# The retention layer's gate projection as seven half-size products per weight block, laid between the heads' products

## The reference, cut to what matters

```python
z = hn @ od_w_in[j]
q, k, v, g = _split(z, OD_SPLIT)          # widths 1024, 1024, 2048, 2048
...
    inner = jnp.einsum("bihd,bjhd->bhij", qc, kc) * decay_intra[None]
    o_inner = jnp.einsum("bhij,bjhe->bihe", inner, vc)
...
o = ((o - mu) * lax.rsqrt(var + GN_EPS)).reshape(b_, s_, h_ * dv) * gn_g.astype(jnp.float32)
y = jax.nn.silu(g.astype(jnp.float32)) * o
...
mix = yc @ od_w_out[j]
h = h + mix
h = h + hier_moe(rms_norm(h, ffn_norm_g[i]), ...)
```

## Time and profile before

| | |
|---|---|
| time, median of 3 runs | 1332.78 us (1332.29 to 1334.24) |
| the profiled execution: time, span of its instructions | 1333.76 us, 1332.0 us |
| PE busy | 1051.0 us (79%) |
| DVE busy | 439.2 us (33%) |
| ACT, POOL busy | 177.8 us (13%), 91.9 us (7%) |
| chain that ended last | DMA 49%, PE 45%, DVE 2% |
| all DMA | 474.88 MB, mean 357 GB/s |

### The profile page before, as it was taken

One profiled execution on the slowest core, in us unless ns is written; L12 is line 12 of the kernel. 1 busy time (PEld: TensorE's weight loads), 2 busy tenths in 40 slices (PEclk: granted clock), 3 DMA queues, 4 the chain that ended last, 5 costly groups with the idle time before them and its releaser, 6 DMA issues.

```text
span 1332.0 us, 26354 instructions
## 1 busy us (share of the span) xinstructions
PE 1051.0 (79%) x10946; PEld 625.6 (47%) x10946; DVE 439.2 (33%) x914; ACT 177.8 (13%) x418; POOL 91.9 (7%) x228
## 2 busy tenths in 40 slices
PE   6999987666676667769999999988666766766678
PEld 5885444333343334434688554544333333333343
DVE  1698522112111111226674547423111211111117
ACT  2334311001000000012121000221000000000011
POOL 0110011000000000000110000011000000000000
PEclk9999999888888888899999999999888888888899
DMA  9945899999999999999454336799999999999992
GB/s 357 322 172 222 336 412 425 429 429 427 430 427 431 428 430 429 427 418 380 167 188 142 113 126 241 300 419 426 430 427 428 429 428 430 427 430 428 427 423 105
DMA packets 57840, 474.88 MB, mean 357 GB/s; under 512 B 4056, under 2 KB 6104, under 8 KB 32192
## 3 DMA queue, kind: packets, MB, share of 16 engines
q1 hardware_dynamic: 56800, 470.32, 85.6%
q10 hardware_dynamic: 768, 2.57, 0.5%
q0 software_dynamic: 224, 1.31, 0.3%
HBM read 473.12 MB, written 3.16 MB: 358 GB/s over the span
## 4 chain that ended last, share of the span: by engine, by line
DMA 49%; PE 45%; DVE 2%; issue 1%; ACT 1%; SPq 1%; POOL 0%; DVEq 0%; ACTq 0%; POOLq 0%
DMA big<-in_moe_w_up_dram 49%; PE ps L935 10%; PE ps L675 7%; PE ps L1121 5%; PE ps L700 5%; PE ps L666 3%; PE ps L1034 3%; PE ps L745 2%; PE ps L656 2%; PE ps L957 1%; PE ps L965 1%; PE ps L846 1%; SPq L540 1%; PE ps L863 1%; DVE big L1797 0%
## 5 line engine op out<-in xcount | busy, mean ns | idle before, releaser
L935 PE MATMUL ps<-big 128*32 128x256 f32 x4064 | 321.7, 484 | 160.1 <-DMA big<-in_moe_w_up_dram 159.9
L935 PEld LDWEIGHTS ps<-big 128*32 128x32 f32 x4064 | 165.9, 138 | 310.6 <-issue 182.4
L1793 DVE SCALAR_TENSOR_TENSOR big<-big,ps 64x256 f32<-64x256 f32 x64 | 26.4, 413 | 682.1 <-ACT big L1356 682.1
L957 PE MATMUL ps<-big 128*32 128x256 f32 x2048 | 123.8, 382 | 57.7 <-DVE big L1802 57.7
L957 PEld LDWEIGHTS ps<-big 128*32 128x32 f32 x2048 | 59.9, 109 | 107.9 <-DVE big L1802 74.8
L965 PE MATMUL ps<-big 32*128 32x256 f32 x1024 | 73.3, 398 | 41.8 <-ACT big L1367 40.6
L1356 ACT ACTIVATE big<-ps 64x256 f32<-64x256 f32 x64 | 24.1, 377 | 566.6 <-PE ps L935 566.6
L675 PE MATMUL ps<-big,xT 128*128 128x512 f32 x224 | 98.1, 592 | 0.0
L965 PEld LDWEIGHTS ps<-big 32*128 32x128 f32 x1024 | 49.5, 184 | 70.8 <-issue 70.8
L2228 POOL TENSOR_TENSOR big<-big,rk 128x64 f32<-128x64 f32 x64 | 18.8, 294 | 769.1 <-PE ps L944 741.9
L905 PE MATMUL ps<-xn,big 128*32 128x256 f32 x1056 | 69.3, 379 | 0.0
(11 more groups left out here) (253 smaller groups left out, 1031.5 us busy)
## 6 DMA issues: line engine op xcount, KB each, us to landing
big<-in_moe_w_gate_dram SPq DMA_DIRECT2D x64, 2048.0 KB, 33.1
big<-in_moe_w_down_dram SPq DMA_DIRECT2D x62, 2048.0 KB, 38.6
big<-in_moe_w_up_dram SPq DMA_DIRECT2D x60, 2048.0 KB, 37.3
big<-in_od_w_in_dram SPq DMA_DIRECT2D x12, 2048.0 KB, 13.4
big<-in_ev_w_in_dram SPq DMA_DIRECT2D x6, 2048.0 KB, 20.7
big<-in_ple_w_gate_dram SPq DMA_DIRECT2D x8, 1024.0 KB, 22.2
big<-in_od_w_out_dram SPq DMA_DIRECT2D x4, 2048.0 KB, 7.9
big<-in_moe_w_up_dram SPq DMA_DIRECT2D x6, 1024.0 KB, 35.5
```

Source lines behind the costliest of these rows:

```text
L935: ins = nc.tensor.matmul(ps[TOK * i:TOK * i + TOK, 5, 0:2 * P].rearrange("p (b n) -> p b n", b=2), xe[:, k, :], (low if k < KD // 2 else w ...
L957: ins = nc.tensor.matmul(ps[TOK * q:TOK * q + TOK, 7, 0:QD], hidT[:, k, :], wd[:, k, q * QD:(q + 1) * QD], start=k == 0, stop=k == KF - 1)
```

## The change

1. Each gate block is computed by the same seven products as the blocks of `SEVEN`: `rg{c}_a` and so on, each four matmuls of 256 columns. In the first of a block's two head steps stand `a, b, d`, in the second `c, a2, b2, c2`. `rg0_a` and `rg0_b` stand ahead of the loop.
2. `GATE_LAG` and `BACK_LAG` become 1 and 3, so the loop has 11 steps, not 12.
3. Banks are fixed in the loop: 4 to 7 for the gate products, 0 for every `ret`, 1 and 2 for `ro`, 3 (and once 0) for `yT`.
4. VectorE gets four weight differences per block. `rg_first` stands behind the value products, `rg_second` between a head's statistics and its scaling, the other two at the end of the block's first step. `rg_part` and `rg_sums` add the products. The gated rows of a block move to the first step of the next block, one half ahead of the head's scaling and one behind it, and now read both operands from SBUF.
5. ScalarE copies four products per block out of PSUM and makes tanh from SBUF.
6. `S4` moves to another place, since it must live through the loop. `S1` to `S3` stay.
7. The first tile and sums of the output projection are made in the loop's step 9, behind the last gated rows.

```diff
+RG_STEPS = ("a", "b", "d"), ("c", "a2", "b2", "c2")
...
-GATE_LAG, BACK_LAG = 2, 4
+GATE_LAG, BACK_LAG = 1, 3
...
+    jobs += ["rg0_a", "rg0_b"]
...
-        jobs += [f"rg{n // 2}_{n % 2}"] if 0 <= n < NH else []
+        jobs += [f"rg{n // 2}_{i}" for i in RG_STEPS[n % 2] if n or i == "d"] if 0 <= n < NH else []
...
+        fixed |= {f"rg{c}_{i}": 4 + "abdc".index(i[0]) for c in range(4) for i in PRODUCTS}
+        fixed |= {f"ret{i}": 0 for i in range(NH)} | {f"ro{i}": 1 + i % 2 for i in range(NH)}
+        fixed |= {f"yT{c}_{t}": 0 if (c, t) == (3, 1) else 3 for c in range(4) for t in range(NT)}
+        fixed |= {f"last_{i}": b for i, b in zip("abdc", (4, 6, 7, 1))} | {"rout_00": 5, "gain1": 2}
...
-            following = 4 if name == "ret0" else following
...
-        S4 = view(15872, HALF, P)
+        S4 = pT[:, 0, :, :].rearrange("p k s -> p (k s)").rearrange("p (k s) -> p k s", k=HALF)
+        RT2 = view(4096, HALF, VD)
+        rg_kept = [[view(12288 + VD * i, VD) for i in range(4)]] + [[view(o1, VD) for o1 in (5120, 5376, 7168, 7424)]] * 3
...
+            RELEASE[f"rv{c}"], RELEASE[f"rg{c}"] = f"rv{c}_c2", f"rg{c}_c2"
...
+            def rg_product(c, i):
+                B11, T1, B21, B22 = rg_quarters(c)
+                lhs, rhs = {"a": (A11, B11), "b": (S1, T1), "d": (S2, RT2), "c": (S3, B11), "a2": (A12, B21), "b2": (S4, B22),
+                            "c2": (A22, T1)}[i]
+                tiles = {"b": c + 1, "d": 5 + 3 * c, "c": 6 + 3 * c, "c2": 7 + 3 * c}
+                b = begin(f"rg{c}_{i}")[:, 0:VD]
+                if i in tiles:
+                    pe.wait_ge(rg_tiles, tiles[i])
+                for k in range(HALF):
+                    ins = nc.tensor.matmul(b, lhs[:, k, :], rhs[:, k, :], start=k == 0 and len(i) == 1, stop=k == HALF - 1,
+                                           skip_group_check=True)
+                end(f"rg{c}_{i}", ins)
+            arrived("rg0")
+            rg_product(0, "a")
+            rg_product(0, "b")
             for w in ROTATED:
                 for t in range(NT):
                     taken(pe, f"{w}T_{t}")
...
-                    c, t = divmod(hd - GATE_LAG, 2)
-                    tokens([f"rg{c}_{t}"], slot(arrived(f"rg{c}"), KD, BLK), t)
+                    c, part = divmod(hd - GATE_LAG, 2)
+                    arrived(f"rg{c}")
+                    for i in RG_STEPS[part]:
+                        if (c, i) not in ((0, "a"), (0, "b")):
+                            rg_product(c, i)
...
-            for n in range(8):
-                if n >= 2:
-                    act.wait_ge(gtanh_used, n - 1)
-                name = f"rg{n // 2}_{n % 2}"
-                full(act, name)
-                sc.activation(rota[:, n % 2, 0, :], bank(name), ACT.Tanh, scale=0.5).then_inc(gtanh_ready, 1)
+            act.wait_ge(values_ready, 5)
+            for c in range(4):
+                P1c, P5c, P7c, _ = rg_kept[c]
+                for i, dst in (("a", P1c), ("b", P5c), ("c", P7c)):
+                    copy_out(f"rg{c}_{i}", dst, bank(f"rg{c}_{i}")[:, 0:VD])
+                if c:
+                    act.wait_ge(ret_y_ready, 2 * c - 1)
+                copy_out(f"rg{c}_a2", rota[:, 0, 1, 0:VD], bank(f"rg{c}_a2")[:, 0:VD])
+                taken(act, f"rg{c}_a2")
+                taken(act, f"rg{c}_b2")
+                sc.activation(rota[:, 0, 0, :], rota[:, 0, 1, :], ACT.Tanh, scale=0.5).then_inc(gtanh_ready, 1)
+                taken(act, f"rg{c}_c2")
+                act.wait_ge(rg_corner, c + 1)
+                sc.activation(rota[:, 1, 0, :], rota[:, 1, 1, :], ACT.Tanh, scale=0.5).then_inc(gtanh_ready, 1)
...
+            def rg_first(c):
+                dve.wait_ge(landed[loads.at[f"rg{c}"]], 16 * loads.turn[f"rg{c}"])
+                B11, B12, B21, B22 = rg_quarters(c)
+                ve.tensor_tensor(B12, B12, B11, ALU.subtract).then_inc(rg_tiles, 1)
+            def rg_second(c):
+                B11, T1, B21, B22 = rg_quarters(c)
+                dve.wait_ge(rg_tiles, 4 + 3 * c)
+                ve.tensor_tensor(RT2, B22, T1, ALU.subtract).then_inc(rg_tiles, 1)
+            def rg_third_and_fourth(c):
+                B11, T1, B21, B22 = rg_quarters(c)
+                dve.wait_ge(rg_tiles, 5 + 3 * c)
+                full(dve, f"rg{c}_a")
+                ve.tensor_tensor(B11, RT2, B11, ALU.subtract).then_inc(rg_tiles, 1)
+                full(dve, f"rg{c}_b")
+                ve.tensor_tensor(T1, B21, RT2, ALU.subtract).then_inc(rg_tiles, 1)
+            def rg_part(c):
+                P1c, _, _, U2 = rg_kept[c]
+                taken(dve, f"rg{c}_a")
+                full(dve, f"rg{c}_d")
+                emptied(f"rg{c}_d", ve.tensor_tensor(U2, P1c, bank(f"rg{c}_d")[:, 0:VD], ALU.add))
+            def rg_sums(c):
+                _, P5c, P7c, U2 = rg_kept[c]
+                taken(dve, f"rg{c}_b")
+                taken(dve, f"rg{c}_c")
+                v(ve.tensor_tensor(P5c, P5c, P7c, ALU.add))
+                taken(dve, f"rg{c}_d")
+                v.sync()
+                ve.tensor_tensor(rota[:, 1, 1, VD:2 * VD], U2, P5c, ALU.add).then_inc(rg_corner, 1)
+                for i, dst in (("b2", rota[:, 0, 1, VD:2 * VD]), ("c2", rota[:, 1, 1, 0:VD])):
+                    full(dve, f"rg{c}_{i}")
+                    emptied(f"rg{c}_{i}", ve.tensor_tensor(dst, U2, bank(f"rg{c}_{i}")[:, 0:VD], ALU.add))
+            def gated_rows(c, t):
+                dve.wait_ge(gtanh_ready, 2 * c + t + 1)
+                v(ve.scalar_tensor_tensor(out=rota[:, t, 1, :], in0=rota[:, t, 0, :], scalar=1.0, in1=rota[:, t, 1, :],
+                                          op0=ALU.add, op1=ALU.mult))
+                for g in (2 * c, 2 * c + 1):
+                    taken(dve, f"ro{g}")
+                cols = ro[:, t, c * 512:(c + 1) * 512]
+                v.sync()
+                ve.tensor_tensor(cols, cols, rota[:, t, 1, :], ALU.mult).then_inc(ret_y_ready, 1)
...
+                else:
+                    rg_first(m - 2)
...
+            rg_second(0)
             for hd in range(HEAD_STEPS):
+                block_n, part = divmod(hd - GATE_LAG, 2)
...
+                if part == 0 and block_n > 0:
+                    gated_rows(block_n - 1, 0)
+                if part == 1 and 0 <= block_n < 3:
+                    rg_second(block_n + 1)
+                if 0 < hd <= NH:
                     dve.wait_ge(gn_root, g + 1)
...
-                n = hd - GATE_LAG
-                if 0 <= n < NH:
-                    c, t = divmod(n, 2)
-                    name = f"rg{c}_{t}"
-                    dve.wait_ge(gtanh_ready, n + 1)
-                    emptied(name, ve.scalar_tensor_tensor(out=rota[:, n % 2, 1, :], in0=rota[:, n % 2, 0, :],
-                                                          scalar=1.0, in1=bank(name), op0=ALU.add, op1=ALU.mult))
-                    taken(dve, name)
-                    dve.sem_inc(gtanh_used, 1)
-                    for g in (2 * c, 2 * c + 1):
-                        taken(dve, f"ro{g}")
-                    cols = ro[:, t, c * 512:(c + 1) * 512]
-                    ve.tensor_tensor(cols, cols, rota[:, n % 2, 1, :], ALU.mult).then_inc(ret_y_ready, 1)
-                if hd == NH:
+                if part == 0 and block_n > 0:
+                    gated_rows(block_n - 1, 1)
+                if part == 0 and block_n < 4:
+                    rg_third_and_fourth(block_n)
+                    rg_part(block_n)
+                if part == 1 and 0 <= block_n < 4:
+                    rg_sums(block_n)
+                if hd == NH + GATE_LAG:
                     out_arrived("rout0", "rout1")
                     out_tile(1, 0, 0)
-                if hd == NH + GATE_LAG:
                     out_parts(0)
                 n = hd - BACK_LAG
                 if 0 <= n < NH:
```

More of the change, by code:

```diff
@@ L362, in trunk @@
         out_read = sem("out_read")
+        rg_tiles, rg_corner = sem("rg_tiles"), sem("rg_corner")
         bank_full = [sem(f"bank_full{i}") for i in range(BANKS)]
@@ L413, in trunk @@
         gn_ready, gn_root = sem("gn_ready"), sem("gn_root")
-        gtanh_ready, gtanh_used, ret_y_ready = sem("gtanh_ready"), sem("gtanh_used"), sem("ret_y_ready")
+        gtanh_ready, ret_y_ready = sem("gtanh_ready"), sem("ret_y_ready")
         ro_ready = sem("ro_ready")
@@ L469, in trunk @@
         for c in range(4):
-            RELEASE[f"rv{c}"], RELEASE[f"rg{c}"] = f"rv{c}_c2", f"rg{c}_1"
+            RELEASE[f"rv{c}"], RELEASE[f"rg{c}"] = f"rv{c}_c2", f"rg{c}_c2"
         for c in range(2):
@@ L479, in quarters, with rg_quarters @@
             w = held(loads.at[SEVEN[m]], KD, BLK)
+            return [w[:, HALF * i:HALF * i + HALF, VD * j:VD * j + VD] for i in range(2) for j in range(2)]
+        def rg_quarters(c):
+            w = slot(f"rg{c}", KD, BLK)
             return [w[:, HALF * i:HALF * i + HALF, VD * j:VD * j + VD] for i in range(2) for j in range(2)]
```

## The result

The changed kernel takes 1326.24 us, median of four runs (1324.2 to 1326.81), against 1332.8 for four runs of the kernel before (1332.29 to 1334.24): a ratio of 0.9946, 95% interval 0.9929 to 0.9964. It is faster, as forecast, by more than the 5.3 us forecast: 6.6 by the medians, 7.2 by the ratio (4.8 to 9.5). Taken together with the rounds of e1 and e2, 13 timings of the kernel before and 9 of the change have means of 1332.5 and 1326.4: 6.1 us apart, give or take 1.

What follows compares the result with a forecast made beforehand. TensorE's queue was taken to bound 729.4 to 853.7, full DMA engines the second mixture. TensorE's 6.6 less 1.0 lost in block 0 and 0.3 later gave 5.3: 1332.78 to 1327.5 us, range 1325.9 to 1330.0.

Steps and rivals of the forecast that it cites:

- That TensorE's time passes to the end: Whatever TensorE saves between 729.4 and 853.7 moves SyncE's last loads, the full DMA stretch and the end equally.
- the rival in which the saving is absorbed: Loads, not TensorE, decide when the DMA engines are full, so nothing moves: 1332.8; absorbed or nearly, chance 0.09.
- TensorE's work, 6.6: Gate blocks in the head steps: seven half-size products cost 12.09 instead of 13.74 us, 6.6 less over four blocks.
- The queue of bank waits, 0.3: Ahead of `ret0`: some twenty semaphores to wait on, costing TensorE 0.3 us, bounds 0 and 0.4.
- `ret1`, 1.0: Block 0: `ret1` waits 1.0 us for bank 0, until VectorE's inner of `ret0` is done.
- `rg0_c`, 0.8 to 1.0: Block 0: `rg0_c` waits 0.8 to 1.0 us for the third weight difference, made only after `ro0`'s scaling.
- The waits in blocks 1 to 3, 0.3: TensorE's waits for VectorE's third difference in the later blocks, 0.3 us in all, with GpSimd's root not hidden.
- Nothing added, VectorE ahead throughout: Rival: no waits in blocks 1 to 3, saving 5.6 to 6.0, time 1327.0; within the forecast's range, no separate chance.
- the rule that the prediction took from the Trainium skill: VectorE and GpSimd share a port pair, locked for a whole instruction when the VectorE one has two SBUF inputs.
- The lead: VectorE's third difference is ready before TensorE wants it: 0.84 us in blocks 1 and 2, 0.19 in block 3.
- The rival of VectorE as the bound: VectorE bounds the head-step loop: at 17.5 us per block 2.3 are lost, time 1329.5; chance 0.21.
- the case that had been given 0.02: Whole kernel: more than 6.3 us saved, beyond the forecast's saving of 4.5 to 6.3; chance 0.02.

Runs made afterwards that it cites:

- e1: Changed kernel with `rg0_d` between `ret0` and `ret1` and block 0's third weight difference made ahead of the loop; 1324.19 us, median of five.
- e2: The changed kernel as it is, timed again in the same rounds as e1; 1326.22 us, ratio 0.9955 to the kernel before.
- e9: The kernel before, unchanged, run once more to look at the start of the program; 1331.86 us, one run.
- e10: The kernel of e1, unchanged, run once more to look at the start of the program; 1325.12 us, one run.
- e3: Changed kernel with only block 0's third weight difference made ahead of the loop; 1327.13 us, one run.
- e11: The kernel of e3, unchanged, run once more to look at the start of the program; 1325.34 us, one run.
- e4: Changed kernel with `rg0_a` and `rg0_b` inside the loop, behind `ro0`, instead of ahead of it; 1329.22 us, one run.
- e5: Changed kernel with only `rg0_d` moved between `ret0` and `ret1`, the third weight difference left in place; 1328.84 us, one run.
- e6: Changed kernel with one more, unused VectorE operation of 1.13 us per block, ahead of the third weight difference; 1327.24 us, one run.
- e7: Changed kernel with three more, unused VectorE operations per block, ahead of the third weight difference; 1344.0 us, one run.
- e8: Changed kernel with the next block's second weight difference made behind the scaling instead of ahead of it; 1327.2 us, one run.

## Why the prediction was right in sign and short in size

The parts of the time, from the profiles (us):

```
                        rv3_c2 ends   stretch   from there to the end
before                     729.40      82.41      520.2
before, e9                 728.25      82.40      519.5
change                     727.59      76.26      521.2
change, e2                 726.67      76.25      524.3
e1                         728.34      74.32      521.0
e1's kernel, e10           728.25      74.32      520.6
e3                         729.84      75.30      520.2
e3's kernel, e11           727.77      75.30      520.3
e4                         727.74      79.05      520.7
e5                         729.80      77.00      520.3
e6                         727.35      78.37      519.8
e7                         728.98      92.32      520.9
e8                         728.38      76.26      520.8
```

**That TensorE's time passes to the end** was right. The last column is the span less the start of the projection's second product. That start moves from 802.57 to 821.30, and the column stays within 519.5 to 521.2 but for one value, e2's, whose 3.1 more stand in its last 46 us. This refutes the rival in which the saving is absorbed.

**TensorE's work, 6.6.** Right: 82.41 less the 1.2 of waits is 81.2, 76.26 less 1.75 is 74.5, and the difference is 6.7.

**The queue of bank waits, 0.3.** This term failed. Measured 0: `rg0_a` and `rg0_b` stand ahead of it and hide it, as they hide the wait for VectorE's last sum. e4, without them, has the 0.98 of before back. The prediction let the two products cover that wait and then priced the queue once more.

**`ret1`, 1.0, and `rg0_c`, 0.8 to 1.0.** Measured 0.87 and 0.88. Both right in cause, as e1, e3 and e5 show. Adding them up was right too, for the second was reckoned from the end of `ro0`. What does not add up is taking them away one at a time (e5). With the queue at 0, block 0's waits were 1.75 in all, not 2.2, and the loss against before 0.55, not 1.0.

**The waits in blocks 1 to 3, 0.3.** Measured 0, and here the mechanism failed: "Whoever comes second waits, so the 0.69 is not hidden: 0.5 to 0.7 is added per step". In the odd step GpSimd came second, and it was GpSimd that lost: its row, expected to start only at the neighbour's end, starts 0.17 into it and is 1.06 long, its result is there before VectorE wants it, and VectorE's operations keep their 0.69. In these steps, which decide when the third difference is done, the root is hidden, whole. The value came from the earlier trace rows, where GpSimd had begun first, with an operation of 512 columns. The order at this place is the reverse, and GpSimd's operation has two columns. The two operations of the gated rows, 1.43 together, cover a root of 1.06. In the even step the root does show: VectorE waits 0.59 for it, instead of 0.80 before. There the "0.5 to 0.7" is about right, but no product waits for that step. The prediction had named this outcome as its last rival, "Nothing added, VectorE ahead throughout", worth 5.6 to 6.0.

On the rule that the prediction took from the Trainium skill (page "SBUF — State Buffer", section "SBUF: two separate sides"), whichever operation starts first keeps the port pair for the whole instruction and the other is blocked. GpSimd's rows agree as far as they go: 742.51 + 1.60 is 0.55 behind the end of L2085 (743.56), and 766.51 + 1.06 is 0.54 behind the end of L2119 (767.03), as if 0.55 of its work began then. L2125, though, starts at 767.16 inside GpSimd's row, which ends at 767.57, and takes 0.69, as the same operation does at 769.49 with GpSimd idle; a lock for the whole row does not show there. This row also says that the order alone is not the answer, for GpSimd's row had begun 0.65 before it. Whether the small size of GpSimd's operation spared VectorE, no run shows: none varied it.

**The lead** was put at 0.84 and 0.19 and then cut to 0.1 and -0.5. Measured it is 1.1 and 0.44 (e6), 0.25 more than the uncut numbers. Of that 0.2 is the gated halves, 1.43 each (766.34 to 767.77) with their wait instructions, where the prediction had 1.52 and took up to 0.3 off besides. From `rg1_c` to `rg2_c` (755.69 to 772.55, 16.86 us) VectorE is busy 14.48, where the prediction had 16.5, or 15.2 without the 1.3 for roots that were not hidden; the 62.5 of the whole stretch also hold the projection's first tiles and sums. The rival of VectorE as the bound falls with this and with e6: one more operation first uses up a lead.

**Sum by its own steps:** 6.7 - 0.55 - 0 = 6.15, where the forecast had 6.6 - 1.0 - 0.3 = 5.3. Of the missing 0.85 us, 0.45 lay in the waits of block 0 (0.3 of it the queue, the rest nearly all `ret1`), 0.3 in those of blocks 1 to 3 and 0.1 in the work.

**The rest of the measured 6.6 to 7.2.** The timed ratios allow 4.8 to 9.5 and, in e2's rounds, 4.3 to 7.9 (1332.51 x 0.0032 and x 0.0059; 6.0 in the middle), so 6.15 fits both, and the means of the 13 and 9 timings of both rounds differ by the same 6.1. Taken from the 1332.8, 6.15 gives 1326.65, inside the forecast's range; that the ratio came out beyond it, in the case that had been given 0.02, is, as far as these means tell, chance. In the profiles `rv3_c2` ends anywhere from 726.7 to 729.8, with no order by kernel. The change's two values are among its lowest. Whether 1 us of that is the kernel's is left open, and with it the cause of what lies beyond 6.15; the comparison by stretches does not depend on it.

The fastest kernel run is e1's, 1324.19 and 1325.12: its two moves take the change's last two waits away, and TensorE does not idle in the head steps.

## What to carry to other kernels

Before adding up two waits in a chain, ask whether the second is measured from the first: filling the first can lengthen the second by more (e5), while filling the second alone pays (e3) and filling both pays in full (e1). A price for two engines at one port holds for the order and the sizes at which it was read, and a delayed result costs nothing as long as the engine that wants it has other work: here 1.43 us of it over a root of 1.06. And compare kernels by the stretch between two events that both have: here it repeats to 0.01 us, while two spans of one kernel differ by 0.5 to 2.2, and single timings of the change run from 1324.2 to 1328.94.

## What the runs showed of the hardware

- TensorE's clock fell to the lower level (0.52 to 0.54) after idle times of 0.98 and 1.89 with 0.7 of work between them (e4), after 4.26 and after 2.30 (e7, 0.52 in both); after 2.95 the next product read 0.64 (e7). It stayed at 1.00 after another 2.30 (e7), after 2.60 (e5), and after 0.87 and 0.88 (the change). A wait so cost 1.7 us more than its length.
- A product that restarts after a wait has a row 0.08 to 0.11 longer (1.97 for 1.89, 0.70 for 0.59), even after a gap of 0.04 (e6).
- The first 64 matmuls take 14.05 to 16.33 us (e4) in 13 profiles of programs that do the same there, and in two of one program 15.74 and 14.05.
- A GpSimd operation of 128x2 takes 0.69 us alone, 1.06 beside a VectorE operation of 0.69 and 1.60 beside one of 1.22 that had begun 0.17 earlier; alone again (e8) it is back at 0.69. VectorE's rows keep their length.
